# Two half-height correction products made full height, and an earlier split of the next head's operands

## What is computed

```python
# MLA: 512 queries, 512 keys and 256 keys of the context, 8 heads, 128 + 64 features per head
scores = (q_nope @ k_nope.T + q_rope @ k_rope.T) * 192 ** -0.5     # k_rope is one for all heads
o = softmax(scores) @ v                                            # then * silu(gate) and @ w_out
# Hyena filter: hdn is 512 x 64, w_out 64 x 4096
h = (hdn @ w_out) * exp(-t * deltas)
```

## Time and profile before

| | |
|---|---|
| median of 3 runs | 2131.43 us (2130.62 to 2136.81) |
| profiled execution | 2124.47 us |
| its span, first to last instruction | 2122.7 us |
| instructions | 24638 |
| granted TensorE clock, mean over the span | 0.984 |

### The profile page before, as it was taken

One profiled execution on the slowest core, in us unless ns is written; L12 is line 12 of the kernel. 1 busy time (PEld: TensorE's weight loads), 2 busy tenths in 40 slices (PEclk: granted clock), 3 DMA queues, 4 the chain that ended last, 5 costly groups with the idle time before them and its releaser, 6 DMA issues.

```text
span 2122.7 us, 24638 instructions
## 1 busy us (share of the span) xinstructions
PE 2028.8 (96%) x9878; PEld 1658.0 (78%) x9878; DVE 1380.2 (65%) x1972; ACT 825.8 (39%) x1270; POOL 232.4 (11%) x238
## 2 busy tenths in 40 slices
PE   8999999999999999999999999999999799999887
PEld 6888887888888888888888887777776576768676
DVE  4577766875785577567558645555545678787774
ACT  4333334331333455444234334433333353444442
POOL 2133321000000100100000010000001213020201
PEclk9999999999999999999999999999999899999998
DMA  5211113434332310243434332101002222233221
GB/s 184 70 50 55 55 50 102 160 132 159 130 122 80 103 41 30 80 158 132 163 114 149 106 112 80 50 31 40 30 30 73 75 70 95 80 104 104 71 90 50
DMA packets 55010, 191.61 MB, mean 90 GB/s; under 512 B 6000, under 2 KB 6320, under 8 KB 54768
## 3 DMA queue, kind: packets, MB, share of 16 engines
q1 hardware_dynamic: 54896, 190.04, 26.6%
HBM read 187.92 MB, written 2.10 MB: 90 GB/s over the span
## 4 chain that ended last, share of the span: by engine, by line
PE 77%; DVE 14%; ACT 5%; issue 3%; POOL 2%; DMA 0%; SPq 0%; DVEq 0%; ACTq 0%
PE PS L325 20%; PE PS L329 19%; PE PS L328 19%; DVE wlo L1803 2%; PE PS L437 2%; PE PS L899 2%; PE PS L332 1%; PE PS L335 1%; PE PS L336 1%; PE PS L888 1%; PE PS L650 1%; PE PS L874 1%; PE PS L387 1%; PE PS L691 1%; DVE hl_h L2470 1%
## 5 line engine op out<-in xcount | busy, mean ns | idle before, releaser
L325 PE MATMUL PS<-nhi,whi 128*128 128x512 f32 x1456 | 601.6, 413 | 27.3 <-DVE nlo L1840 8.1
L329 PE MATMUL PS<-nhi,wlo 128*128 128x512 f32 x1456 | 574.4, 395 | 0.0
L328 PE MATMUL PS<-nlo,whi 128*128 128x512 f32 x1456 | 573.6, 394 | 0.0
L1803 DVE TENSOR_TENSOR wlo<-raw,whi 128x1024 fp32r<-128x1024 f32 x291 | 361.7, 1248 | 194.3 <-ACT whi L1185 193.6
L1185 ACT ACTIVATE whi<-raw 128x1024 fp32r<-128x1024 f32 x291 | 304.3, 1052 | 206.2 <-PE PS L325 191.0
L325 PEld LDWEIGHTS PS<-nhi,whi 128*128 128x128 f32 x1456 | 277.6, 191 | 101.1 <-issue 18.5
L329 PEld LDWEIGHTS PS<-nhi,wlo 128*128 128x128 f32 x1456 | 277.0, 190 | 60.5
L328 PEld LDWEIGHTS PS<-nlo,whi 128*128 128x128 f32 x1456 | 278.1, 191 | 52.7 <-issue 2.6
L2623 POOL TENSOR_TENSOR diag<-diag,sqb 128x512 f32<-128x512 f32 (+1 forms) x56 | 72.9, 1301 | 1169.7 <-ACT sqb L1194 1087.1
L325 PE MATMUL PS<-hh_f,whi 128*128 128x512 f32 x352 | 137.9, 392 | 0.0
L328 PE MATMUL PS<-hl_f,whi 128*128 128x512 f32 x352 | 137.7, 391 | 0.0
(11 more groups left out here) (357 smaller groups left out, 3423.4 us busy)
## 6 DMA issues: line engine op xcount, KB each, us to landing
raw<-in_stream SPq DMA_DIRECT2D x291, 512.0 KB, 3.5
aw_f<-in_ada SPq DMA_DIRECT2D x48, 512.0 KB, 4.4
dc<-in_decay SPq DMA_DIRECT2D x4, 1024.0 KB, 5.5
hT<-in_xT SPq DMA_DIRECT2D x8, 256.0 KB, 7.1
out<-hT SPq DMA_DIRECT2D x8, 256.0 KB, 2.0
ctx_f<-in_ctx SPq DMA_DIRECT2D x1, 1024.0 KB, 7.7
ab_h<-in_filt_out SPq DMA_DIRECT2D x8, 128.0 KB, 2.9
mask<-in_masks SPq DMA_DIRECT2D x1, 512.0 KB, 8.5
```

What stands on the lines that cost most here:

```text
L325: op = e.matmul(out, hi, xh, start=first, stop=False)
L328: e.matmul(out, hi, xl, start=False, stop=False)
L329: return e.matmul(out, lo, xh, start=False, stop=last)
L1803: e.tensor_tensor(m.wlo[:, c % HL, :], m.raw[:, c % RAW, :], m.whi[:, c % HL, :].bitcast(F), SUB).then_inc(*s.w_lo.tick(c))
```

## The change

Three edits, apart from the signals' names.

1. Line 874 multiplies all 128 rows of `qr` (high and low part) by all 128 rows of `krl`. The product lo·lo is added.
2. `hdl` gets 128 partitions; DVE writes the low part twice, by two instructions in place of one; line 1011 multiplies it by all 128 rows of `ws`, which adds lo·lo. PE and SP wait for the second of the two.
3. In `proj`, ACT rounds `qn` and `kn` in the step in which DVE multiplies them by the norm (before: `qn` after one more step and a yield, `kn` one step later still). DVE subtracts for `qn` in that same step (before: three steps later) and for `kn` two steps later (before: four). The number of steps is the same.

```diff
-        a.hd, a.hdl = p("hd", [128, T], FR), p("hdl", [64, T], FR)
+        a.hd, a.hdl = p("hd", [128, T], FR), p("hdl", [128, T], FR)
...
-            p = slice(64 * x, 64 * x + 64)
...
-                op = e.matmul(b[:, 0:n], a.qr[p, y, x, c], a.krl[p, ks], start=False, stop=True)
+                op = e.matmul(b[:, 0:n], a.qr[:, y, x, c], a.krl[:, ks], start=False, stop=True)
...
-                    q.wait_ge(*s.made_v.at("hdl"))
+                    q.wait_ge(*s.made_v.at("hdl", 1))
...
-                    e.matmul(B[4 + x], a.hdl[:, cs], f.ws[0:64, i % 2, :], start=False,
+                    e.matmul(B[4 + x], a.hdl[:, cs], f.ws[:, i % 2, :], start=False,
...
             w.tiles(1)
             w.tiles(1)
-            yield
-            yield from w.steps(1)
             q.wait_ge(*s.taken_v.at("qn", h))
             e.activation(a.qn[:, z, 0, :], a.tq[:, :], ACT.Copy).then_inc(*s.made_a.tick("qn", h))
-            yield from w.steps(1)
             q.wait_ge(*s.taken_v.at("kn", h, 1))
             e.activation(a.kn[:, z, 0, 0:T], a.tk, ACT.Copy).then_inc(*s.made_a.tick("kn", h, 0))
             e.activation(a.kn[:, z, 0, T:], a.tkc, ACT.Copy).then_inc(*s.made_a.tick("kn", h, 1))
-            yield from w.steps(KD - 2)
+            yield
+            yield from w.steps(KD)
...
-            yield
-            yield from w.steps(2)
             q.wait_ge(*s.made_a.at("qn", h))
             e.tensor_tensor(a.qn[:, z, 1, :], a.tq[:, :], a.qn[:, z, 0, :].bitcast(F), SUB).then_inc(*s.made_v.tick("qn", h))
+            yield
             yield from w.steps(1)
             q.wait_ge(*s.made_a.at("kn", h, 1))
...
-            yield from w.steps(KD - 3)
+            yield from w.steps(KD - 1)
...
-            e.tensor_tensor(m.hy.hdl[:, :], fa[:, 1, :], m.hy.hd[0:64, :].bitcast(F), SUB).then_inc(*s.made_v.tick("hdl"))
+            for x in range(2):
+                e.tensor_tensor(m.hy.hdl[64 * x:64 * x + 64, :], fa[:, 1, :], m.hy.hd[0:64, :].bitcast(F),
+                                SUB).then_inc(*s.made_v.tick("hdl", x))
```

## The result

| | before | changed |
|---|---|---|
| median of runs beside each other | 2131.02 us (2129.73 to 2136.81) | 2112.19 us (2110.29 to 2112.84) |
| ratio, 95% interval | | 0.9905 (0.9886 to 0.9924) |
| span of the profiled execution | 2122.7 us | 2108.5 us |
| granted clock, mean | 0.984 | 0.982 |

The change is 18.8 us faster by the medians, 16 to 24 us by the interval; 18.1 us were forecast. The two profiled spans differ by 14.2 us only: the profiled execution of before is among the fastest of its kernel, with a granted clock of 0.984, and of the 45 runs of before beside the experiments the four at 0.984 took 2124.9 to 2125.9 us, those at 0.981 to 0.983 took 2126.9 to 2131.8, and those at 0.979 and 0.980 took 2132.7 to 2136.3.

The account below looks back on a forecast made before the run. PE was taken as the bound, busy 96% of the span with 77% of the chain. 22.8 us (128-row products) - 3.0 (earlier split) - 1.7 (clock) = 18.1, off the 2131.4 median: 2113 us, range 2100 to 2122.

Parts of the forecast that it names:

- Price of the height: Score product, line 874: going to 64 rows and back costs PE 0.78 us per block, 25.0 us over 32.
- the first rival: Products of 64 rows: height costs nothing, only the earlier split counts, -2.2 us, so 2134 us; chance 0.06.
- What PE gives back: Places where PE already waits: 2.3 us before even heads, 2.3 at their first projection, 0.8 at the last head.
- Even heads: First scores of even heads: PE's wait for DVE's low part of `kn` goes, 1.15 x 3 heads = 3.4 us gained.
- Odd heads: ACT's rounding of `kn` waits for `tkc` ahead of the probabilities' copy; PE's value products wait, 4 x 1.6 = 6.4 us lost.
- part 2: The earlier split of `qn` and `kn` in ACT's and DVE's queues: +3.4 - 6.4 = -3.0 us.
- Filters: Filter product, line 1011: PE saves 12.8 us, a quarter counts, 3.2 us; bounds 0 and 12.8.
- Clock: Filter stages: longer PE waits bring one new stretch of half clock, -1.7 us; bounds 0 and 5 us.
- more is given back: No filter gain, 5 us to the clock, ACT's wait costs in even heads too: 10 us gain, 2121; chance 0.13.
- hardly anything is given back: ACT's wait short or covered, PE sets the filter stages more: 31 us gain, 2100; chance 0.22.
- Slower: ACT's wait for `tkc` pushes a block's whole softmax chain in odd heads, 8 us each: 2137; chance 0.04.

Follow-up runs that it names:

- both_low: The kernel before, with line 873 also 64 rows high, leaving out the query's low part times the key's high part; 2128.83 us, ratio 0.9992.
- scores_high: The kernel before with only the score product (line 874) made 128 rows high; 2111.64 us, ratio 0.9921.
- both_high: The kernel before with score and filter products 128 rows high and the old order of the splits; 2108.40 us, ratio 0.9905.
- even_only: The changed kernel with the old order of the splits back in odd heads, the earlier split kept in even heads; 2103.78 us, ratio 0.9874.
- filters_high: The kernel before with only the filter product (line 1011) and `hdl` made 128 rows high; 2126.80 us, ratio 0.9990.

## Why the prediction was right

The mechanism was right: the change of height, what DVE's waits take back, and the loss in the odd heads. That 18.1 lies so near 18.8 is in part luck: the interval of the gain is 16 to 24 us, and two misses of over 1 us go opposite ways. In the attention part 16.6 us were forecast (25.0 - 5.4 - 3.0), and 15.4 came. Behind it 1.5 us were forecast (3.2 - 1.7), and 2.8 came if the traces with either height of the filter product are averaged.

- *Price of the height.* 25.0 us on PE for 32 blocks. Rows 3 and the changed kernel's timeline give the same, and both_low shows that it is the change of height. Right, and the first rival is refuted.
- *What PE gives back.* Before even heads, behind `tq`, 2.3 us were forecast; the step to the gate's first matmul grew from 0.17 to 0.95 us, three times 0.78. For the first projection of even heads it was 2.3 us too; PE waits 1.7 us more there (2.4 for 0.7). At the last head 0.8 us were forecast, and 0.6 more waiting came, but at another place than was read: the wait of 2.64 us did not grow, that for the low part of the outputs just before it (L2355) grew from 0.8 to 1.4. One place was missed: in the first head the transposes now wait 0.7 us for the scaling (3.3 us in two waits, where the earlier trace rows had 2.6 in one). This is most of why scores_high brought 18.4 us in its stage and not 19.6.
- *Even heads.* 3.4 us from the low part of `kn` made earlier. In both_high, with the old order, the waits for it stand at 3.0 us in three; in the changed kernel they are gone. Right.
- *Odd heads.* 6.4 us worked out as four waits of 1.6. Measured: four of 1.42, 5.7 us, and 6.8 us of the attention part between the changed kernel and even_only. The sum along ACT's queue came out too: the copy was put 0.86 us behind the end of `tkc` (0.03 + 0.52 + 0.31), and starts 0.88 behind it (1371.82 + 0.41 to 1373.11). Right, and it decided the sign of part 2: -3.0 us forecast, -3.1 measured between both_high and the changed kernel.
- *Filters.* 3.2 us of 12.8 were taken, by a count of the products that DVE waits for. The runs of filters_high give 0 to 4.5 us, and the traces with 128 rows have a Hyena part 2.8 us shorter in the mean than those with 64. The reason given (DVE has its own queue) holds; the size agrees, but the count of two products in eight is not shown. The waits of the earlier trace rows grew less than the 2 to 3 us that were taken: 1.80, 1.62 and 1.89 us became 2.00, 1.66 and 2.39.
- *Clock.* 1.7 us were taken for one new stretch of half clock. Between the two traces the granted clock over the Hyena part fell from 0.97 to 0.95 (rows below), which is more than one stretch, and that part took 368.4 us for 367.5. But the other kernels with the filter product of 64 rows need 371 to 374 us for it, and over whole runs the clock is the same, 0.982 for most runs of before and 0.982 or 0.983 for the changed kernel's. So this term is not confirmed; its cost can't be parted from the filters' term.

One stretch each of before and of the changed kernel: span; busy us of PE, PEld, DVE, ACT and POOL; granted clock; DMA:

```profile
1660.00:2030.00 370.00, 336.93 (x1518) 262.11 (x1517) 281.50 (x391) 158.99 (x243) 74.65 (x56) 0.97 0.25 84
```

```profile
1645.00:2016.00 371.00, 330.48 (x1517) 268.55 (x1517) 281.64 (x391) 158.80 (x243) 74.70 (x56) 0.95 0.26 84
```

The traces' sum is 15.4 us in the attention part, and 14.2 over the span; the medians say 18.8. The difference of 4.6 us goes with the granted clock of the profiled execution of before: it had 0.984, where 0.982 is the most common, and 0.002 of 2125 us are 4 us (an estimate from these numbers). Its Hyena part is 3.5 us below the mean of the four. Single executions differ by as much in parts that no edit touches: the start of the attention part lies at 1358.2 us in before and at 1364.5 in filters_high, whose code up to there is the same.

The prediction's rivals "more is given back" (2121) and "hardly anything is given back" (2100) are both outside the runs. "Slower" needed 6.6 us per odd head; it was 1.4 by the wait, 1.7 by the attention part.

## What to carry to other kernels

Look at the distance from start to start around a product that is less high than its neighbours: if an operand that lies twice anyway lets it have their height, both changes are saved, and here a product more accurate than needed is the cheaper one. A rounding that is moved forward on a copying engine waits for its input in front of everything queued there; count that queue to its end before moving it, head by head: here the same move gained 1.1 us in each even head and cost 1.4 in each odd one. The timelines put that down to the chunk split in front of the input, which only the odd heads have; no run moved the split. And time saved on the busiest engine counts only up to the next place where it waits already: list these waits first, then subtract. A stage read from one trace has the clock of that one execution; compare it with the same stage of several before calling a small term nothing.

## What the runs showed of the hardware

A change between 128 and 64 rows costs 0.2 us on PE, some 0.10 before the first product of the new height and 0.10 behind it, with 256 as with 512 columns, and a second product of 64 rows behind the first costs nothing more. The Trainium skill, TensorEngine Tiling (Array Packing), section Key Properties, calls it a drain and gives no duration; these are the numbers of this chip.

The clock fell in the changed kernel where it had not before: behind two waits of 1.00 and 1.79 us close together, matmuls of 512 columns follow each other at 0.43 us in place of 0.23, and the granted clock from 1699.6 to 1706.0 us is 0.50, the lower of the two levels (1.2 and 2.4 GHz). In before the waits there are 0.70 and 1.79 us, and the distances behind them stay 0.23. In scores_high, whose filter product is untouched, they are 1.48 and 1.79, and the distances 0.43: the fall does not need the filters' edit. Timelines of PE, first of the changed kernel, then of before:

```profile
1698.43 0.33 PE L1034 MATMUL PS<-ident,zf 128*128 128x128 f32 x1 [1.00 <-DVE zf L2492]
1700.55 0.47 PE L1034 MATMUL PS<-ident,zf 128*128 128x128 f32 x1 [1.79 <-DVE zf L2492]
...
1702.10 0.63 PE L325 MATMUL PS<-nhi,whi 128*128 128x512 f32 x1
1702.53 0.63 PE L328 MATMUL PS<-nlo,whi 128*128 128x512 f32 x1
```

```profile
1712.61 0.33 PE L1035 MATMUL PS<-ident,zf 128*128 128x128 f32 x1 [0.70 <-DVE zf L2494]
1714.73 0.33 PE L1035 MATMUL PS<-ident,zf 128*128 128x128 f32 x1 [1.79 <-DVE zf L2494]
...
1716.29 0.40 PE L325 MATMUL PS<-nhi,whi 128*128 128x512 f32 x1
1716.52 0.39 PE L328 MATMUL PS<-nlo,whi 128*128 128x512 f32 x1
```
